# Difference attention in a two-block network: 64-row score matmuls of two units in one group, and the first softmax division on the output

## The chip, the cores and the metric

One core of a Trainium2 chip runs the whole network in one launch. The metric is the device time of that core in microseconds (us). TensorE (PE in the profile) multiplies, VectorE (DVE) and ScalarE (ACT) do the elementwise work, GpSimd (POOL) some sums, and SyncE (SP) issues the transfers of weights.

## What is computed

The program is a block of first kind (feed-forward, RWKV time mix, dilated attention, feed-forward) and then two layers of a second kind, each with an mLSTM branch, a difference attention branch, a Fourier branch, and a feed-forward. The change touches the difference attention branch of the two layers alone:

```python
def _diff_attn_core(q, k, v, lam):
    s = jnp.einsum('bqhmd,bkhmd->bhmqk', q, k).astype(jnp.float32) * (DA_DH ** -0.5)
    p = jax.nn.softmax(s, axis=-1)
    a = p[:, :, 0] - lam * p[:, :, 1]
    return jnp.einsum('bhqk,bkhe->bqhe', a.astype(v.dtype), v)
```

There are 8 heads of 2 x 64 columns of queries and keys (m = 0 and 1) and 128 columns of values. 256 tokens x attend to all 512 keys (x and context); in layer 0 the 256 context tokens attend to the 256 context keys too. All is float32.

## The kernel before, in words

Each engine has its own hand-written program; they meet at semaphores. A `Tally` counts them: `t.wait(name)` waits for one more count, `t.step(ins)` and `t.out(ins, name)` issue an instruction, raise a semaphore and wait for it, so that each engine goes strictly in its written order.

A unit is one head and one block of 128 queries (`units`). Layer 0 has 32 units, in which key widths of 512 and 256 alternate (query blocks 0, 2, 1, 3 of a head); layer 1 has 16 units, all 512 wide. For each unit n:

- PE, `da_scores`: two matmuls with 64 rows, m = 0 on rows 0 to 63 into bank n % 2, m = 1 on rows 64 to 127 into bank 4 + n % 2. They raise "scores". Before unit n they wait for "probs_in" of unit n - 2, which read the same banks.
- DVE, `da_in`: two maxima over the row (L3801) and a scaling by -0.125 (L3802), "weights_out".
- ACT, `exp` for m = 0 and m = 1 (L2725): the exponential out of PSUM into `DA_P`, with the row's sum by an accumulator read. After m = 1, "probs_in".
- DVE, `da_mid`: reciprocal of both sums (L3810), second weights by its reciprocal and by the factor lambda (L3811), first weights by theirs, plus the second (L3812), "probs".
- PE, `da_turn`: 4 or 2 transposes into bank 2 (L1143), "pt_psum". ACT, L2746: the copy of it out of bank 2, "pt_ready". PE, `da_values`: 4 or 2 matmuls into bank 6 + n % 2, "pv_psum". DVE, L3822: the copy of the 128x128 output, "pv_out".

A float32 matmul has two records in the profile, so "x4" of the scores is one unit, and x8 with x4 are the values and transposes of a 512-wide unit. Between these steps PE makes matmuls of the next gate (`fill`, one of 512 columns in layer 0, two of 256 in layer 1 per unit; 4 tiles in all, drained by ACT at L2341). PE's order in step n: scores n, fill, values n - 3, transposes n - 2. DVE's: `da_in` n, `da_mid` n - 1, copy n - 3. ACT's: exp(n, 0), copy of the transposes n - 2, exp(n, 1). Ahead of the loop stands the last product of the value projection (`end_units`, 16 records of 256 columns), which PE makes behind the scores of unit 0; ACT writes out its last tile and loads the exponential's table before exp(0, 0). Behind the loop PE waits for the last copy of the output before it goes on, and DVE and ACT normalize the output.

Of the kernel before, what the change touches and what calls it, by code (L numbers as in the profile page):

```python
# [18 lines left out]
P = 128  # L19
# [517 lines left out]
def program(nc, x_in, ctx_in, wide_in, down_in, par_in, const_in, const1_in, const2_in, out, dbg=None):  # L537
    with ExitStack() as ctx:
# [33 lines left out]
        bank = [ctx.enter_context(nc.psum_tensor(f"bank{b}", [P, 512], F32)) for b in range(8)]  # L572
# [562 lines left out]
        def _(pe):  # L1135
# [322 lines left out]
            def end_units(keys):  # L1458
                product(keys[-1], "P4")
# [444 lines left out]
            for la in range(2):  # L1904
# [122 lines left out]
                def da_scores(n):  # L2027
                    h, q = units[n]
                    k0, k1 = keys_of(q)
                    if n >= 2:  # L2030
                        t.wait("probs_in")
                    for m in range(2):
                        rows = slice(64 * m, 64 * m + 64)
                        last = matmul(bank[4 * m + n % 2][:, 0:(k1 - k0) * P], qT[rows, h, q * P:(q + 1) * P], kT[rows, h, k0 * P:k1 * P])
                    last.then_inc(S["scores"], 1)
# [23 lines left out]
                for n in range(len(units) + 3):  # L2059
                    if n == 0:  # L2060
                        pe.wait_ge(S["act_out"], ST[p + "da_v"].act_end - 1)
                    if n < len(units):
                        da_scores(n)
                        if n == 0:
                            end_units(run)
                        fill(per)
                    if n >= 3:
                        da_values(n - 3)
                    if 2 <= n < len(units) + 2:
                        da_turn(n - 2)  # L2070
# [125 lines left out]
        def _(act):  # L2196
# [438 lines left out]
            for la in range(2):  # L2635
# [86 lines left out]
                def exp(n, m, w):  # L2722

                    sc = stat[:, 4 * (n % 3):4 * (n % 3) + 4]
                    ins = af(DA_P(n, m)[:, 0:w], bank[4 * m + n % 2][:, 0:w], ACT.Exp, scale=0.125, bias=sc[:, m:m + 1],  # L2725
                             accum_out=sc[:, 2 + m:3 + m])
                    if m == 0:
                        t.step(ins)
                    else:
                        t.out(ins, "probs_in")  # L2730

                for n in range(n_units + 2):
                    if n < n_units:
                        w = 512 if DA_ORDER[qtiles][n % qtiles] < 2 else 256
                        if (n + 1) % (n_units // 4) == 0:
                            tile = (n + 1) // (n_units // 4) - 1
                            filled(ST[p + "da_gate0"], tile, DA_GATES0[:, tile, 0:nq], bank[3][:, 0:nq])
                        t.wait("weights_out")
                        exp(n, 0, w)
                    if n >= 2:  # L2740
                        k = n - 2
                        w = 512 if DA_ORDER[qtiles][k % qtiles] < 2 else 256
                        t.wait("pt_psum")
                        if k >= 2:
                            act.wait_ge(S["pv_psum"], PV_DA[la] + k - 1)
                        t.out(af(DA_PT(k)[:, 0:w], bank[2][:, 0:w], ACT.Copy), "pt_ready")  # L2746
                    if n < n_units:
                        exp(n, 1, 512 if DA_ORDER[qtiles][n % qtiles] < 2 else 256)
                act.wait_ge(S["act_out"], ST[p + "da_gate0"].act_end)

                def da_squares():
# [126 lines left out]
        def _(dve):  # L2878
# [731 lines left out]
            for la in range(2):  # L3610
# [185 lines left out]
                def da_in(n):  # L3796
                    w = 512 if units[n][1] < 2 else 256
                    sc = stat[:, 4 * (n % 3):4 * (n % 3) + 4]
                    t.wait("scores")
                    for m in range(2):  # L3800
                        t.step(nc.vector.tensor_reduce(sc[:, m:m + 1], bank[4 * m + n % 2][:, 0:w], axis=AX.X, op=ALU.max))  # L3801
                    t.out(ts(sc[:, 0:2], sc[:, 0:2], -0.125, None, mul), "weights_out")  # L3802

                def da_mid(n):

                    w = 512 if units[n][1] < 2 else 256
                    sc = stat[:, 4 * (n % 3):4 * (n % 3) + 4]
                    p0, p1 = DA_P(n, 0)[:, 0:w], DA_P(n, 1)[:, 0:w]
                    t.wait("probs_in")
                    t.step(nc.vector.reciprocal(sc[:, 2:4], sc[:, 2:4]))  # L3810
                    t.step(ts(p1, p1, sc[:, 3:4], lam[:, 2:3], mul, mul))  # L3811
                    t.out(stt(p0, p0, sc[:, 2:3], p1, mul, add), "probs")  # L3812

                for n in range(len(units) + 3):
                    if n < len(units):
                        da_in(n)
                    if 1 <= n < len(units) + 1:
                        da_mid(n - 1)
                    if n >= 3:
                        h, q = units[n - 3]  # L3820
                        t.wait("pv_psum")
                        t.out(copy(y3[:, q, h * P:(h + 1) * P], bank[6 + (n - 3) % 2][:, 0:P]), "pv_out")  # L3822
                say("dve_for_act")
                run = RUNS[2]
                t.wait("act_for_dve")
# [513 lines left out]
```

## Time and profile before

| what | value |
|---|---|
| median of 3 runs | 3066.15 us (3064.68 to 3066.62) |
| span of the profiled execution | 3068.6 us |
| PE, DVE, ACT busy over the span | 2994.5, 1778.7, 598.7 us (98%, 58%, 20%) |
| loop of layer 0 (first scores to last output copy) | 1420.8 to 1525.0 us |
| loop of layer 1 | 2619.2 to 2683.7 us |

The profiled execution has no device time of its own beside its span; the span is 0.08% above the median of the runs. Busy time counts an instruction from its start to its end. Matmuls overlap each other, so their starts tell more than their lengths. In a timeline row "[1.94 <-DVE small L3802]" is the idle time ahead of the instruction and what ended it.

### The profile page before, as it was taken

The page shows a single profiled execution, that of the slowest core. Times are in us where ns is not written, and L with a number is a line of the kernel's source. Part 1 is how long each engine was busy: PE and PEld are TensorE (multiplying, and loading weights), DVE is VectorE, ACT ScalarE, POOL GpSimd, SP SyncE. Part 2 cuts the span into 40 slices and gives each one's busy share as a digit, 9 for nine tenths or more (in the row PEclk, how much of TensorE's full clock was granted, in tenths as well). Part 3 has the DMA queues.
Part 4 walks back from the last instruction along what each step waited for, and adds up shares of the span by engine and source line. Part 5 has one row for each costly group of instructions (what it writes and reads, how often), then busy time and mean ns, then how long its engine had stood idle before and what let it go on. Part 6 is the DMA issues. An engine that isn't in the chain of part 4 may idle for free.

```text
span 3068.6 us, 37635 instructions
## 1 busy us (share of the span) xinstructions
PE 2994.5 (98%) x15352; PEld 2256.1 (74%) x15352; DVE 1778.7 (58%) x2602; ACT 598.7 (20%) x1182; POOL 535.9 (17%) x214
## 2 busy tenths in 40 slices
PE   8999999999999999999999999999999999999998
PEld 4448898775458757887588888888888888678543
DVE  6984642647766556657853268777324513742574
ACT  2103212212121112113611131111021200511110
POOL 4330000023332101221021212211110001010332
PEclk9999999999999999999999999999999999999999
DMA  6663301345543302442021234443232143133453
GB/s 264 234 233 137 138 30 44 123 180 180 181 184 129 112 28 76 144 133 94 29 87 65 83 144 152 150 143 137 98 124 92 60 158 115 58 151 130 162 175 126
DMA packets 57115, 389.86 MB, mean 127 GB/s; under 512 B 9072, under 2 KB 23408, under 8 KB 36336
## 3 DMA queue, kind: packets, MB, share of 16 engines
q1 hardware_dynamic: 52592, 383.27, 34.6%
q10 hardware_dynamic: 4352, 4.20, 0.7%
q8 instruction: 122, 2.00, 0.3%
q14 instruction: 49, 0.40, 0.0%
HBM read 373.53 MB, written 1.05 MB: 122 GB/s over the span
## 4 chain that ended last, share of the span: by engine, by line
PE 85%; DVE 7%; issue 6%; ACT 2%; POOL 0%; DMA 0%; DVEq 0%; SPq 0%; ACTq 0%; POOLq 0%
PE bank L1140 84%; DVE weights L3143 1%; PE bank L1143 1%; DVE arena L3472 0%; DVE factors L3156 0%; DVE factors L3051 0%; ACT h_T L2247 0%; DVE weights L3146 0%; DVE h_T L3245 0%; DVE arena L2990 0%; DVE arena L3173 0%; DVE masks L3941 0%; DVE arena L3506 0%; DVE small L3801 0%; DMA params<-params_dram 0%
## 5 line engine op out<-in xcount | busy, mean ns | idle before, releaser
L1140 PE MATMUL bank<-h_T,weights 128*128 128x256 f32 (+1 forms) x3184 | 780.6, 397 | 14.4 <-ACT arena L2364 3.1
L1140 PEld LDWEIGHTS bank<-h_T,weights 128*128 128x128 f32 x3184 | 601.2, 191 | 151.8 <-issue 65.1
L2862 POOL TENSOR_TENSOR weights<-weights 128x1024 f32<-128x1024 f32 (+2 forms) x105 | 272.5, 2596 | 1290.1 <-DMA weights<-wide_slabs_dram 1191.7
L2873 POOL TENSOR_TENSOR factors<-weights 128x1024 f32<-128x1024 f32 (+2 forms) x105 | 265.5, 2528 | 1214.4 <-PE bank L1140 992.8
L1140 PE MATMUL bank<-arena,weights 128*128 128x256 f32 x1784 | 393.9, 379 | 2.5 <-DVE arena L3173 0.9
L1140 PEld LDWEIGHTS bank<-arena,weights 128*128 128x128 f32 x1784 | 337.9, 190 | 51.4 <-issue 1.8
L1140 PE MATMUL bank<-factors,weights 128*128 128x256 f32 x1432 | 325.4, 381 | 5.0 <-DVE arena L3173 3.9
L1140 PE MATMUL bank<-weights,h_T 128*128 128x256 f32 (+2 forms) x1000 | 323.4, 470 | 4.1 <-DMA weights<-wide_slabs_dram 2.1
L1140 PE MATMUL bank<-weights,factors 128*128 128x256 f32 (+1 forms) x960 | 312.7, 470 | 4.1 <-DVE factors L3156 2.1
L1140 PEld LDWEIGHTS bank<-factors,weights 128*128 128x128 f32 x1432 | 272.7, 191 | 43.7 <-DVE arena L3173 5.1
L1140 PEld LDWEIGHTS bank<-weights,h_T 128*128 128x128 f32 x1000 | 190.3, 191 | 117.9 <-issue 89.8
L3143 DVE TENSOR_TENSOR weights<-weights,factors 128x1024 f32<-128x1024 f32 (+2 forms) x104 | 136.4, 1312 | 232.8 <-PE bank L1140 202.5
L1140 PEld LDWEIGHTS bank<-weights,factors 128*128 128x128 f32 x960 | 181.5, 190 | 118.9 <-issue 98.3
L3146 DVE TENSOR_TENSOR weights<-weights,factors 128x1024 f32<-128x1024 f32 (+2 forms) x104 | 130.4, 1254 | 168.5 <-PE bank L1140 167.0
L2357 ACT ACTIVATE arena<-bank 128x512 f32<-128x512 f32 (+1 forms) x144 | 83.3, 579 | 694.3 <-PE bank L1140 604.8
L1140 PE MATMUL bank<-factors 128*128 128x256 f32 (+3 forms) x816 | 212.7, 413 | 0.0
L3173 DVE TENSOR_TENSOR arena<-bank,arena 128x512 f32<-128x512 f32 (+1 forms) x132 | 88.1, 667 | 195.1 <-PE bank L1140 192.2
L1140 PE MATMUL bank<-arena 64*64 64x64 f32 (+7 forms) x1544 | 176.5, 307 | 11.0 <-ACT arena L2746 6.4
L1140 PEld LDWEIGHTS bank<-factors 128*128 128x128 f32 (+1 forms) x816 | 148.9, 190 | 50.6 <-issue 33.8
L1140 PE MATMUL bank<-weights,arena 128*128 128x512 f32 x396 | 175.0, 593 | 4.6 <-DVE weights L3143 4.6
L1140 PEld LDWEIGHTS bank<-arena 64*64 64x64 f32 (+2 forms) x1544 | 124.9, 162 | 52.9 <-issue 23.8
L3941 DVE SCALAR_TENSOR_TENSOR masks<-arena 128x1024 f32<-128x1024 f32 x88 | 152.5, 1732 | 2.9
(392 smaller groups left out, 2693.7 us busy)
## 6 DMA issues: line engine op xcount, KB each, us to landing
weights<-wide_slabs_dram SPq DMA_DIRECT2D x143, 2048.0 KB, 7.8
arena<-wide_slabs_dram SPq DMA_DIRECT2D x61, 512.0 KB, 4.2
weights<-down_slabs_dram SPq DMA_DIRECT2D x8, 1408.0 KB, 5.8
merged_T<-arena SPq DMA_DIRECT2D x240, 32.0 KB, 1.9
merged_T<-wide_slabs_dram SPq DMA_DIRECT2D x15, 512.0 KB, 4.5
x_T<-wide_slabs_dram SPq DMA_DIRECT2D x11, 512.0 KB, 9.3
arena<-arena ACTq DMA_DIRECT2D x16, 256.0 KB, 10.1
weights<-wide_slabs_dram SPq DMA_DIRECT2D x3, 1024.0 KB, 5.1
```

The lines of the kernel that those rows point to most:

```text
L1140: return mm(out, lhsT, rhs, start=start, stop=stop, skip_group_check=True)
L1143: return nc.tensor.transpose(out, in_, ident[0:in_.shape[0], 0:in_.shape[0]])
L2357: af(place(u)[into], bank_of(u, of), ACT.Copy, scale=scale).then_inc(S["snapped"], 1)
L2862: nc.gpsimd.tensor_tensor(b[2], b[2], b[3], ALU.add).then_inc(S["first_sums"], 1)
L2873: nc.gpsimd.tensor_tensor(e, b[2], b[0], ALU.subtract).then_inc(S["first_sums"], 1)
L3143: ins = tt(b[0], b[3], e, sub)
L3146: ins = tt(b[1], b[1], e, sub)
L3173: ins = stt(dst, src, 1.0 / 16, dst, mul, add) if "ml_k" in u.name else tt(dst, src, dst, add)
L3941: ins = stt(ADA_PRODUCT, ada_tile(b), 1.0, COND_ROWS[:, s * D:(s + 1) * D], mul, mul, accum_out=ada_all[:, column:column + 1])
```

## The change

PE issues the scores of units n and n + 1 (n even) in one group, and waits for "probs_in" of both units before (n - 2 and n - 1) ahead of the group. At the start both first units stand ahead of `end_units`. ACT makes exp(n, 0) and exp(n, 1) one behind the other, and the copy of the transposes n - 2 behind them; the drain of a gate tile moves behind the exponentials too. DVE makes `da_in` of two units, then an output copy, `da_mid` of the two, and another output copy. In `da_mid` the multiplication of the whole second weights (L3811) goes; in its place comes an operation on one column (lambda times the second reciprocal times the first sum), and the addition takes that column as its factor. The output is divided by the first sum in its copy out of PSUM (tensor_scalar in place of copy); the reciprocals lie in 6 places of `stat` until then.

```diff
--- before.py
+++ after.py
@@ -2027,8 +2027,6 @@
                 def da_scores(n):
                     h, q = units[n]
                     k0, k1 = keys_of(q)
-                    if n >= 2:
-                        t.wait("probs_in")
                     for m in range(2):
                         rows = slice(64 * m, 64 * m + 64)
                         last = matmul(bank[4 * m + n % 2][:, 0:(k1 - k0) * P], qT[rows, h, q * P:(q + 1) * P], kT[rows, h, k0 * P:k1 * P])
@@ -2060,9 +2058,13 @@
                     if n == 0:
                         pe.wait_ge(S["act_out"], ST[p + "da_v"].act_end - 1)
                     if n < len(units):
-                        da_scores(n)
-                        if n == 0:
-                            end_units(run)
+                        if n % 2 == 0:
+                            if n:
+                                t.wait("probs_in", 2)
+                            da_scores(n)
+                            da_scores(n + 1)
+                            if n == 0:
+                                end_units(run)
                         fill(per)
                     if n >= 3:
                         da_values(n - 3)
@@ -2732,11 +2734,12 @@
                 for n in range(n_units + 2):
                     if n < n_units:
                         w = 512 if DA_ORDER[qtiles][n % qtiles] < 2 else 256
+                        t.wait("weights_out")
+                        exp(n, 0, w)
+                        exp(n, 1, w)
                         if (n + 1) % (n_units // 4) == 0:
                             tile = (n + 1) // (n_units // 4) - 1
                             filled(ST[p + "da_gate0"], tile, DA_GATES0[:, tile, 0:nq], bank[3][:, 0:nq])
-                        t.wait("weights_out")
-                        exp(n, 0, w)
                     if n >= 2:
                         k = n - 2
                         w = 512 if DA_ORDER[qtiles][k % qtiles] < 2 else 256
@@ -2744,8 +2747,6 @@
                         if k >= 2:
                             act.wait_ge(S["pv_psum"], PV_DA[la] + k - 1)
                         t.out(af(DA_PT(k)[:, 0:w], bank[2][:, 0:w], ACT.Copy), "pt_ready")
-                    if n < n_units:
-                        exp(n, 1, 512 if DA_ORDER[qtiles][n % qtiles] < 2 else 256)
                 act.wait_ge(S["act_out"], ST[p + "da_gate0"].act_end)
 
                 def da_squares():
@@ -3807,19 +3808,29 @@
                     sc = stat[:, 4 * (n % 3):4 * (n % 3) + 4]
                     p0, p1 = DA_P(n, 0)[:, 0:w], DA_P(n, 1)[:, 0:w]
                     t.wait("probs_in")
-                    t.step(nc.vector.reciprocal(sc[:, 2:4], sc[:, 2:4]))
-                    t.step(ts(p1, p1, sc[:, 3:4], lam[:, 2:3], mul, mul))
-                    t.out(stt(p0, p0, sc[:, 2:3], p1, mul, add), "probs")
-
-                for n in range(len(units) + 3):
+                    t.step(nc.vector.reciprocal(da_rows(n), sc[:, 2:4]))
+                    t.step(stt(sc[:, 3:4], da_rows(n)[:, 1:2], lam[:, 2:3], sc[:, 2:3], mul, mul))
+                    t.out(stt(p0, p1, sc[:, 3:4], p0, mul, add), "probs")
+
+                def da_rows(n):
+                    return stat[:, 16 + 2 * (n % 6):18 + 2 * (n % 6)]
+
+                def da_out(n):
+                    h, q = units[n]
+                    t.wait("pv_psum")
+                    t.out(ts(y3[:, q, h * P:(h + 1) * P], bank[6 + n % 2][:, 0:P], da_rows(n)[:, 0:1], None, mul), "pv_out")
+
+                for n in range(0, len(units) + 4, 2):
                     if n < len(units):
                         da_in(n)
-                    if 1 <= n < len(units) + 1:
-                        da_mid(n - 1)
-                    if n >= 3:
-                        h, q = units[n - 3]
-                        t.wait("pv_psum")
-                        t.out(copy(y3[:, q, h * P:(h + 1) * P], bank[6 + (n - 3) % 2][:, 0:P]), "pv_out")
+                        da_in(n + 1)
+                    if 3 <= n < len(units) + 3:
+                        da_out(n - 3)
+                    if n < len(units):
+                        da_mid(n)
+                        da_mid(n + 1)
+                    if 2 <= n < len(units) + 2:
+                        da_out(n - 2)
                 say("dve_for_act")
                 run = RUNS[2]
                 t.wait("act_for_dve")
```

The places on which the prediction rests, as the programs stand. PE in layer 0, from the first scores (banks 0 and 4 are the scores of a 512-wide unit, banks 1 and 5 of a 256-wide one, bank 3 the fill or `end_units`, bank 2 transposes, banks 6 and 7 values). Before:

```order
L1140 MATMUL bank3<-h_T,weights 128x512
L1140 MATMUL bank6<-arena 128x128 x4
L1143 MATMUL bank2<-common,arena 128x128 x2
L1140 MATMUL bank0<-arena 128x512
L1140 MATMUL bank4<-arena 128x512
L1140 MATMUL bank3<-h_T,weights 128x512
L1140 MATMUL bank7<-arena 128x128 x2
L1143 MATMUL bank2<-common,arena 128x128 x4
L1140 MATMUL bank1<-arena 128x256
L1140 MATMUL bank5<-arena 128x256
```

and now:

```order
L1140 MATMUL bank0<-arena 128x512
L1140 MATMUL bank4<-arena 128x512
L1140 MATMUL bank1<-arena 128x256
L1140 MATMUL bank5<-arena 128x256
L1140 MATMUL bank3<-h_T,weights 128x512
L1140 MATMUL bank7<-arena 128x128 x2
L1143 MATMUL bank2<-common,arena 128x128 x4
L1140 MATMUL bank3<-h_T,weights 128x512
L1140 MATMUL bank6<-arena 128x128 x4
L1143 MATMUL bank2<-common,arena 128x128 x2
```

Here a matmul is one row, not two records. The same ten stand in one pair of units; the scores of the second have moved ahead by a fill, values and transposes.

ACT in layer 0, from the table load (banks 0 and 4, then 1 and 5, are read by the exponentials; bank 2 by the copy of the transposes). Before:

```order
L2725 ACT_TABLE_LOAD
L2725 ACTIVATE arena,small<-bank0,small 128x512
L2725 ACTIVATE arena,small<-bank4,small 128x512
L2725 ACTIVATE arena,small<-bank1,small 128x256
L2725 ACTIVATE arena,small<-bank5,small 128x256
L2725 ACTIVATE arena,small<-bank0,small 128x512
L2746 ACTIVATE arena<-bank2 128x512
L2725 ACTIVATE arena,small<-bank4,small 128x512
L2725 ACTIVATE arena,small<-bank1,small 128x256
L2746 ACTIVATE arena<-bank2 128x256
L2725 ACTIVATE arena,small<-bank5,small 128x256
```

and now:

```order
L2727 ACT_TABLE_LOAD
L2727 ACTIVATE arena,small<-bank0,small 128x512
L2727 ACTIVATE arena,small<-bank4,small 128x512
L2727 ACTIVATE arena,small<-bank1,small 128x256
L2727 ACTIVATE arena,small<-bank5,small 128x256
L2727 ACTIVATE arena,small<-bank0,small 128x512
L2727 ACTIVATE arena,small<-bank4,small 128x512
L2749 ACTIVATE arena<-bank2 128x512
L2727 ACTIVATE arena,small<-bank1,small 128x256
L2727 ACTIVATE arena,small<-bank5,small 128x256
L2749 ACTIVATE arena<-bank2 128x256
```

The copy of the transposes has moved from between the two exponentials of a unit to behind them, so one copy stands between the exponentials of the two units of a group.

## Rows read from the trace of the kernel before

**Rows 1.** Busy time by engine in the two loops; columns as printed, clock as share.
```profile
core 0: us, PE busy (x) PEld busy (x) DVE busy (x) ACT busy (x) POOL busy (x), PEclk, DMA share, GB/s
1420.80:1525.10 104.30, 99.50 (x497) 56.19 (x497) 90.04 (x227) 62.11 (x166) 2.49 (x1) 1.00 0.11 41
2619.20:2683.80 64.60, 60.26 (x337) 41.35 (x336) 52.18 (x114) 37.79 (x86) 0.00 (x0) 1.00 0.18 66
```

**Rows 2.** Timeline (start us, us, engine, line, operation), layer 0, one pair.
```profile
1479.02 1.42 DVE L3801 TENSOR_REDUCE small<-bank 128x1 f32<-128x512 f32 x2
...
1480.59 0.70 PE L1140 MATMUL bank<-arena 64*128 64x256 f32 x4
...
1481.22 1.13 PE L1140 MATMUL bank<-h_T,weights 128*128 128x512 f32 x2
...
1484.94 0.69 DVE L3801 TENSOR_REDUCE small<-bank 128x1 f32<-128x512 f32 x1
```

**Rows 3.** Timeline, layer 0, first units of the loop.
```profile
1427.54 0.69 ACT L2725 ACTIVATE arena<-bank,small 128x512 f32<-128x512 f32 x1
...
1429.18 1.13 PE L1140 MATMUL bank<-arena 64*128 64x512 f32 x4
...
1429.40 0.47 ACT L2725 ACTIVATE arena<-bank,small 128x256 f32<-128x256 f32 x1 [0.27 <-DVE small L3802]
...
1430.00 0.47 ACT L2725 ACTIVATE arena<-bank,small 128x256 f32<-128x256 f32 x1
...
1430.79 1.41 DVE L3801 TENSOR_REDUCE small<-bank 128x1 f32<-128x512 f32 x2
...
1432.50 0.69 ACT L2725 ACTIVATE arena<-bank,small 128x512 f32<-128x512 f32 x1 [1.94 <-DVE small L3802]
...
1433.31 0.60 ACT L2746 ACTIVATE arena<-bank 128x512 f32<-128x512 f32 x1
...
1433.94 0.69 ACT L2725 ACTIVATE arena<-bank,small 128x512 f32<-128x512 f32 x1
...
1435.27 0.70 PE L1140 MATMUL bank<-arena 64*128 64x512 f32 x2
```

**Rows 4.** Timeline, layer 1, first units of the loop.
```profile
2625.84 1.13 PE L1140 MATMUL bank<-arena 64*128 64x512 f32 x4
2625.97 0.69 ACT L2725 ACTIVATE arena<-bank,small 128x512 f32<-128x512 f32 x1
...
2627.08 1.42 DVE L3801 TENSOR_REDUCE small<-bank 128x1 f32<-128x512 f32 x2 [4.97 <-PE bank L1140]
...
2627.96 1.13 PE L1140 MATMUL bank<-arena 64*128 64x512 f32 x4
```

**Rows 5.** Timeline of DVE, layer 1, the second half of one unit.
```profile
2638.37 0.17 DVE L3810 RECIPROCAL small<-small 128x2 f32<-128x2 f32 x1
...
2638.57 0.55 DVE L3811 TENSOR_SCALAR arena<-arena,small 128x512 f32<-128x512 f32 x1
...
2639.15 0.75 DVE L3812 SCALAR_TENSOR_TENSOR arena<-arena,small 128x512 f32<-128x512 f32 x1
...
2639.82 0.28 DVE L3822 COPY arena<-bank 128x128 f32<-128x128 f32 x1
```

**Rows 6.** Timeline of PE, an earlier stage: 64-row matmuls of two widths together.
```profile
578.54 0.93 PE L1140 MATMUL bank<-factors 64*128 64x128 f32 x8
579.39 0.70 PE L1140 MATMUL bank<-arena,weights 128*128 128x256 f32 x2
```

**Rows 7.** Timeline of PE and DVE, last score pairs and last output copies.
```profile
1513.34 1.13 PE L1140 MATMUL bank<-arena 64*128 64x512 f32 x4
...
1524.72 0.29 DVE L3822 COPY arena<-bank 128x128 f32<-128x128 f32 x1 [1.16 <-PE bank L1140]
...
2669.36 1.13 PE L1140 MATMUL bank<-arena 64*128 64x512 f32 x4
...
2683.44 0.29 DVE L3822 COPY arena<-bank 128x128 f32<-128x128 f32 x1 [2.04 <-PE bank L1140]
```

**Rows 8.** Busy time by engine around a fall of TensorE's clock; columns as in rows 1.
```profile
390.00:392.00 2.00, 0.85 (x16) 0.61 (x12) 1.93 (x6) 0.00 (x0) 0.00 (x0) 1.00 0.03 8
...
394.20:397.60 3.40, 3.40 (x60) 3.40 (x58) 1.42 (x4) 0.55 (x1) 0.00 (x0) 0.50 0.00 0
```

## The prediction

> **What bounds the kernel now.** I first read the busy times of the two loops [rows 1]. PE is busy 99.5 of 104.3 us in layer 0 and 60.3 of 64.6 us in layer 1, DVE 90.0 and 52.2 us, ACT about 60% of each. So two engines are nearly full, and the loops are a close race. The timeline decides it. In layer 0 a pair of units (512 and 256 keys wide) takes 5.92 us from maximum to maximum on DVE (1479.02 to 1484.94) [rows 2], and DVE has no gap in between: DVE bounds layer 0. In layer 1 the scores of units 2 and 14 start at 2627.96 and 2669.36 [rows 4, 7], 41.40 us for 12 units, 3.45 us for one and 6.90 us for a pair; there PE goes from group to group without a wait and DVE's unit is just as full. Both loops hide all hand-overs between engines behind work of other units. A change that regroups units must keep that cover, so I read the hand-overs too [rows 3, 4].
>
> **What is taken from PE.** A group of two 64-row matmuls of 256 columns takes 0.63 us up to the fill (1480.59 to 1481.22) [rows 2]. Where matmuls of 128 and of 256 columns with 64 rows stand together, both take 0.85 us (578.54 to 579.39) [rows 6]: the 128 wide ones add 0.22, a quarter of the 0.85, where they are a third of the columns. So a second group behind a first pays its columns alone; a group has a fixed 0.2 us (0.63 less twice 0.22). I take 0.2 us as the low end and 0.4 us (as much again at its neighbours, an estimate by doubling) as the high end per group saved. 24 groups go: 4.8 to 9.6 us of PE work. The Trainium skill, page TensorEngine Tiling (Array Packing), section Key Properties, says that a change of the tiling mode drains TensorE; by that rule alone the change can only win, and the time would be that of the first rival below.
>
> **What is taken from DVE.** The scaling of the second weights goes, 0.58 us from its start to the next (2638.57 to 2639.15) [rows 5], in the 256-wide units less. A one-column operation comes; the nearest row is the reciprocal of two columns, 0.20 us to the next start [rows 5]. The output copy (0.28 us [rows 5]) becomes a multiplication by a column; I take it at the same time, and up to 0.07 us more for the range. Net some 0.3 us per unit, 24 x 2 units: 14 us of DVE work. It is worth nothing unless DVE sets the pace, and I find that it no longer does.
>
> **What is added: a longer ring.** Scores of units n and n + 1 now wait until both units before are through both exponentials, and nothing of a later unit is under way in the meantime. I follow the ring from one group's start to the next in layer 0, with n 512 wide and n + 1 256 wide:
>
> - scores of n start, to the first maximum: 1.24 us (2625.84 to 2627.08, DVE was idle) [rows 4];
> - first maximum to the first exponential: 1.71 us (1430.79 to 1432.50, ACT was idle) [rows 3];
> - both exponentials of n, one behind the other: 2 x 0.81 = 1.62 us (1432.50 to 1433.31) [rows 3];
> - the copy of the transposes n - 2, which now stands right here, then values n - 2 and transposes n - 1, and the next scores: 1.96 us (1433.31 to 1435.27, the same shapes in the same order) [rows 3].
>
> The sum is 6.53 us. The other branch of the last step is the copy (0.63, 1433.31 to 1433.94) and the exponentials of n + 1 (2 x 0.60, 1429.40 to 1430.00) [rows 3], about 1.85 us, so values and transposes end last by 0.1. The maximum of n + 1 on DVE ends long before ACT comes to it. PE's and DVE's own work per pair is some 5.5 us, less than the ring. So layer 0 goes from 5.92 to 6.53 us per pair. Group starts from unit 2 to unit 30 are 14 rings, 91.4 us, against 84.2 us before (1429.18 to 1513.34) [rows 3, 7]: **+7.2 us**.
>
> In layer 1 all units are 512 wide, and the ring runs through DVE: exponentials of n, copy, exponentials of n + 1: 1.62 + 0.63 + 1.59 = 3.84 us; a hand-over of 0.1 us (an estimate, the smallest gaps between engines here); reciprocal 0.20, one-column operation 0.20, addition 0.67 (2639.15 to 2639.82), output copy 0.32 [rows 5]; then maximum to exponential, 1.71. That is 7.04 us against 6.90. Six rings give 42.2 against 41.4 us: **+0.8 us**.
>
> **Start and end of the loops.** The first two score groups now stand ahead of the value projection's last product, which delays that product, and by it ACT's table load and exp(0, 0), by 0.43 us in layer 0 (two 64-row steps of 0.22) and by 0.86 us in layer 1, where the unit is 512 wide. Before, scores 2 started at 1429.18 and 2627.96. Now they wait for the exponentials of units 0 and 1: 1427.54 + 0.43 + 1.62 + 1.20 gives 1430.8, and 2625.97 + 0.86 + 3.24 gives 2630.1 [rows 3, 4]: **+1.6 and +2.1 us**. At the end of layer 0, from scores 30 to the last output copy, it was 11.4 us (1513.34 to 1524.72) [rows 7]. Now exp(31) ends after 1.24 + 1.71 + 1.62 + 0.63 + 1.17 = 6.4 us, the gate drain and the copy of transposes 29 (half as wide, 0.2 us shorter) come to 7.4, then values 29 with transposes 30 (1.3 us), a round of 1.96, and copy 31 with values 31 (1.3): 12.0 us, **+0.6**. In layer 1 the same laying out gives 14.0 us against 14.1 (2669.36 to 2683.44) [rows 7]: **0**. PE waits for the last output copy before it goes on, so all of it reaches the end of the program; outside the loops nothing changes.
>
> Sum: 7.2 + 0.8 + 1.6 + 2.1 + 0.6 = 12.3, rounded up for the small terms to 12.5 us. The profiled execution's span of 3068.6 would become 3081; against the median of 3066.15 I say **3078.6 us**.
>
> **The rivals.**
>
> *PE sets the pace, and the change wins.* If ACT's results come before PE asks for them, the pair costs PE 0.4 us less, 5.5 us in layer 0 and 6.5 in layer 1, and DVE is lighter still. Then 24 x 0.4 = 9.6 us go: 3056.6 us. It decides if the ring of layer 0 is below 5.9 us; I find 6.53, each part a start-to-start time. For it speaks that both full engines lose work. Chance 0.08.
>
> *The copy of the transposes does not count.* If it fell into ACT's idle time ahead of the exponentials, the ring would lose 0.63 us: 5.9 in layer 0, 6.4 in layer 1 (there PE's 6.5 decides, a gain of 2.4), and with the longer start the time is about 3068, no difference. Against it: ACT's order is fixed, the transposes n - 2 come behind the group and a fill on PE, later than the first exponential, and at 1433.94 the exponential starts only behind the copy though its unit had long been ready [rows 3]. Chance 0.10.
>
> *PE's clock falls.* Before, the loops ran at a granted clock of 1.00 [rows 1]. At 390 to 392 us PE was busy 0.85 of 2.00 us, and at 394.2 to 397.6 the granted clock was 0.50 [rows 8], the lower level, 1.2 GHz. The new wait ahead of scores 2 leaves PE idle some 2 us in each layer, and in the ring it is busy about five sixths of the time. One such fall costs up to 1.7 us where PE is in the ring; two of them 3.4: 3082. Chance 0.12.
>
> *The second group pays its fixed cost after all.* Then scores n + 1 come 0.2 us later, under the 1.4 us of maxima of unit n: no difference in time, only in the trace.
>
> **How the numbers follow.** My forecast has the rest, 0.70. Slower are the forecast and the clock's case, 0.82; within 0.2% (6.1 us, about what a measurement of this kernel can tell) is the second rival, 0.10; faster the first, 0.08. The range takes in a shorter ring (6.42 by the exponentials' branch alone, -1.5 us) and a start that costs nothing (-3.7) at the low end, and two falls of the clock and a dearer output copy at the high end: 3072 to 3083. Both other cases are below it, 0.18 together.
>
> **What would show it.** Group starts 6.5 us apart in layer 0 and 7.0 in layer 1; PE idle about 1 us ahead of the values (released by ACT's copy) in each pair; DVE waiting for ACT ahead of the second reciprocal; first groups at 1430.8 and some 10 us later than now in layer 1; no L3811 of full width. I am wrong if group starts are under 6.0 us apart in layer 0, and then it is the ring that failed.

## The result, and the profile after

| kernel | median (runs) | ratio to before, 95% interval |
|---|---|---|
| before | 3065.41 us (3063.09 to 3066.93, 6) | |
| changed | 3076.70 us (3072.50 to 3078.59, 6) | 1.0033 [1.0024, 1.0043] |

The change costs 11.3 us by the medians; the ratio of 1.0033 is 10.1 us, with an interval of 7.4 to 13.2. The forecast was 3078.6 us, in a range of 3072 to 3083. The profiled execution of the changed kernel took 3077.47 us. Its page and its two loops:

```profile
span 3075.7 us, 37642 instructions
PE 2987.1 (97%) x15352; PEld 2253.7 (73%) x15352; DVE 1772.6 (58%) x2602; ACT 595.2 (19%) x1182; POOL 534.6 (17%) x214
```

Busy time by engine, one loop a row, columns as in [rows 1]:

```profile
1417.20:1529.00 111.80, 95.06 (x497) 57.23 (x497) 85.21 (x227) 60.27 (x166) 2.35 (x1) 1.00 0.11 38
2624.20:2690.90 66.70, 58.96 (x337) 41.56 (x337) 48.71 (x114) 36.13 (x86) 0.00 (x0) 1.00 0.18 64
```

PE has 4.4 us and DVE 4.8 us less to do in layer 0 than in [rows 1], as meant, and the loop takes 7.5 us longer: both engines now wait. The waits of the layer 0 loop (engine and line, what it waited for, us in total, times, longest) name the place. First before, then after:

```profile
PEld bank L1140 <- ACT arena L2746: 15.1, 19, 1.6
PE bank L1140 <- ACT arena L2746: 3.5, 6, 0.8
```

```profile
PEld bank L1140 <- ACT arena L2749: 26.4, 18, 2.0
...
PE bank L1140 <- ACT arena L2749: 13.3, 18, 1.2
```

PE's wait for ACT's copy of the transposes grew from 3.5 to 13.3 us, that of its weight loads from 15.1 to 26.4 us. One pair of units of layer 0, all engines (start, length, engine, line, operation), shows the ring:

```profile
1452.96 1.56 PE L1140 MATMUL bank<-arena 64*128 64x512 f32 x8
...
1454.20 1.42 DVE L3802 TENSOR_REDUCE small<-bank 128x1 f32<-128x512 f32 x2
...
1454.45 1.13 PE L1140 MATMUL bank<-h_T,weights 128*128 128x512 f32 x2
...
1455.92 0.69 ACT L2727 ACTIVATE arena<-bank,small 128x512 f32<-128x512 f32 x1 [2.42 <-DVE small L3803]
...
1456.73 0.69 ACT L2727 ACTIVATE arena<-bank,small 128x512 f32<-128x512 f32 x1
...
1457.41 0.59 ACT L2749 ACTIVATE arena<-bank 128x512 f32<-128x512 f32 x1
...
1458.05 1.16 PE L1140 MATMUL bank<-arena 128*128 128x128 f32 x8 [0.73 <-ACT arena L2749]
...
1459.29 0.17 DVE L3811 RECIPROCAL small<-small 128x2 f32<-128x2 f32 x1 [0.48 <-ACT arena L2727]
...
1459.35 0.70 PE L1140 MATMUL bank<-arena 64*128 64x512 f32 x2
```

From group to group it is 6.39 us (1452.96 to 1459.35). Its legs: scores to maximum 1.24, maximum to exponential 1.72, both exponentials 1.49, and from the copy by way of the values to the next group 1.94. The other way to that group, through the exponentials of the 256-wide unit, was ready some 0.1 us earlier: in experiment 4, where PE waits for them, the group starts 0.62 us behind the start of the last of them (1472.21 to 1472.83), which here would be 1458.62 + 0.62 = 1459.24 where the group starts at 1459.35. It is a close race. PE stands idle 0.73 us ahead of the values and DVE 0.48 us ahead of the second reciprocal. The start and the end of the loops, layer 0 and then layer 1:

```profile
1417.19 1.56 PE L1140 MATMUL bank<-arena 64*128 64x512 f32 x8
...
1427.04 1.56 PE L1140 MATMUL bank<-arena 64*128 64x512 f32 x8 [1.91 <-ACT arena L2727]
...
1516.91 1.56 PE L1140 MATMUL bank<-arena 64*128 64x512 f32 x8
...
1528.56 0.35 DVE L3821 TENSOR_SCALAR arena<-bank,small 128x128 f32<-128x128 f32 x1 [1.10 <-PE bank L1140]
...
2624.25 1.99 PE L1140 MATMUL bank<-arena 64*128 64x512 f32 x8
...
2634.96 1.99 PE L1140 MATMUL bank<-arena 64*128 64x512 f32 x8 [2.33 <-ACT arena L2727]
...
2676.74 1.99 PE L1140 MATMUL bank<-arena 64*128 64x512 f32 x8
...
2690.45 0.35 DVE L3821 TENSOR_SCALAR arena<-bank,small 128x128 f32<-128x128 f32 x1 [1.98 <-PE bank L1140]
```

From here on "the loops" are the times from the first scores to the last output copy of each layer, and "a pair" is the time between the scores of units n and n + 2 (n even, so 512 wide in layer 0). They are read from the profiled execution of each kernel:

| kernel | pair, layers 0 / 1 | loops, layers 0 / 1 | sum against before |
|---|---|---|---|
| before | 5.92 / 6.90 | 103.91 / 64.20 | |
| changed | 6.40 / 7.01 | 111.37 / 66.20 | +9.5 |

The spans of the two profiled executions differ by 7.1 us only, since the one of before came to its first scores 3.6 us later (1420.81 against 1417.19) over the same instructions. That is why the loops are compared, and the medians, but not the spans.

### The profile page after: what moved, and what is told of

Its sections match the earlier page's. It is cut to its first block, busy times and chain, and to the rows that moved or that the text cites. A ratio compares the mean times of both kernels' runs of the same rounds, so it can differ in the third digit from the quotient of the medians.

```text
span 3075.7 us, 37642 instructions
## 1 busy us (share of the span) xinstructions
PE 2987.1 (97%) x15352; PEld 2253.7 (73%) x15352; DVE 1772.6 (58%) x2602; ACT 595.2 (19%) x1182; POOL 534.6 (17%) x214
## 4 chain that ended last, share of the span: by engine, by line
PE 43%; issue 5%; DVE 1%; ACT 1%; POOL 0%; DVEq 0%; ACTq 0%; POOLq 0%
PE bank L1140 43%; ACT h_T L2249 0%; DVE masks L3952 0%; DVE factors L3157 0%; DVE weights L3144 0%; POOL factors L2874 0%; PE bank L1143 0%; DVE arena L3174 0%; DVE arena L3856 0%; DVE weights L3147 0%; POOL weights L2863 0%; DVE factors L4041 0%; DVE arena L4037 0%; DVE h_T L2933 0%; DVE arena L3757 0%
## 5 line engine op out<-in xcount | busy, mean ns | idle before, releaser
L1140 PE MATMUL bank<-arena 64*64 64x64 f32 (+7 forms) x1544 | 170.2, 303 | 26.4 <-ACT arena L2749 17.1
## 6 DMA issues: line engine op xcount, KB each, us to landing
arena<-arena ACTq DMA_DIRECT2D x16, 256.0 KB, 10.1
```

Of the source, the lines that this page charges most:

```text
L1140: return mm(out, lhsT, rhs, start=start, stop=stop, skip_group_check=True)
```

## The experiments

The kernel before was run again beside them: its median was 3067.10 us beside experiments 1 to 4 and 3066.60 us beside 5 to 8, and the ratios are against these runs.

What had to be told apart: whether the ring (the theory), PE's work or DVE's work sets the pair; whether the copy of the transposes counts; and which of the change's three parts (PE's grouping, ACT's order, the arithmetic) makes the loss.

**1. The order without the arithmetic.** The changed kernel with the old `da_mid` and the old output copy.

```diff
-                    t.step(stt(sc[:, 3:4], da_rows(n)[:, 1:2], lam[:, 2:3], sc[:, 2:3], mul, mul))
-                    t.out(stt(p0, p1, sc[:, 3:4], p0, mul, add), "probs")
+                    t.step(ts(p1, p1, sc[:, 3:4], lam[:, 2:3], mul, mul))
+                    t.out(stt(p0, p0, sc[:, 2:3], p1, mul, add), "probs")
```

> The changed order on all engines with the old arithmetic (full-width scaling of the second weights, plain output copy). Ring theory (the group waits for exponentials, copy of the transposes, values and transposes, and DVE has slack in layer 0): the added DVE work of about 0.3 us a unit shows in layer 0 for less than 0.1 us a pair (6.40 to about 6.48), in layer 1, where DVE is in the ring, for 0.26 a pair (7.02 to about 7.3); in all 2 to 3 us slower than the change, some 12 to 14 us slower than before. Rival (DVE's total work sets the pace): 48 units x 0.26 = 12 us slower than the change.

Measured: 3077.64 us, ratio 1.0042 [1.0027, 1.0058]; pairs 6.46 and 7.28 to 7.29 us. PE in each layer:

```profile
1469.23 1.56 PE L1140 MATMUL bank<-arena 64*128 64x512 f32 x8
...
1475.69 0.70 PE L1140 MATMUL bank<-arena 64*128 64x512 f32 x2
```

```profile
2647.32 1.99 PE L1140 MATMUL bank<-arena 64*128 64x512 f32 x8
...
2654.60 0.70 PE L1140 MATMUL bank<-arena 64*128 64x512 f32 x2
```

With all of DVE's old work back, the pair grows by 0.06 us in layer 0, where DVE is not in the ring, and by 0.27 in layer 1, where it is. The median is 0.9 us above that of the changed kernel, where the rival wanted 12. So in the new order DVE's work is not the bound of layer 0, and the order alone makes the loss.

**2. The arithmetic without the order.** The changed kernel with the loops of before on PE, ACT and DVE (PE's and ACT's as in before, DVE's `da_in` n, `da_mid` n - 1, output n - 3).

```diff
-                for n in range(0, len(units) + 4, 2):
+                for n in range(len(units) + 3):
                     if n < len(units):
                         da_in(n)
...
+                    if 1 <= n < len(units) + 1:
+                        da_mid(n - 1)
+                    if n >= 3:
                         da_out(n - 3)
```

> The old order on all engines with the new arithmetic. Ring theory: PE's own work bounds both loops, 5.8 us a pair in layer 0 (5.92 before, where DVE was full) and 6.9 in layer 1 as before; 2 to 3 us faster than before, 3062 to 3063. Rival (DVE's work sets the pace): 48 x 0.26 = 12 us faster. Rival (the arithmetic itself, with its column in the output copy, costs the time): slower than before.

Measured: 3063.89 us, ratio 0.9993 [0.9984, 1.0002]; pairs 5.79 and 6.90, loops 101.87 and 63.52. PE in layer 0, from the scores of one 512-wide unit to the next:

```profile
1464.87 1.13 PE L1140 MATMUL bank<-arena 64*128 64x512 f32 x4
...
1470.66 0.70 PE L1140 MATMUL bank<-arena 64*128 64x512 f32 x2
```

PE is idle nowhere in this pair: it takes over as the bound, 0.13 us below DVE's 5.92. The lighter DVE is worth 2.0 us in the loop of layer 0 and 0.7 in that of layer 1, and no more, because PE stands right behind it. The medians alone do not show the gain: their interval holds 1.

**3. A shorter copy, in the changed order.** ACT copies the first 128 columns of the transposes alone. The rest of the copy is left out, so the values of the other columns are stale.

```diff
-                        t.out(af(DA_PT(k)[:, 0:w], bank[2][:, 0:w], ACT.Copy), "pt_ready")
+                        t.out(af(DA_PT(k)[:, 0:P], bank[2][:, 0:P], ACT.Copy), "pt_ready")
```

> The change, but ACT copies only the first 128 columns of the transposes out of PSUM, so values of the other columns are stale. Ring theory: the copy stands in the ring, and 0.3 us less of it (0.63 to about 0.31 for a 512-wide unit) makes the pair 6.4 to 6.1 us in layer 0 and 7.0 to 6.7 in layer 1: 5 us off in layer 0, 2 to 3 in layer 1, 7 to 8 us faster than the change. Rival (the wait for both units' exponentials alone sets the pace, or PE does): no difference.

Measured: 3068.88 us, ratio 1.0010 [1.0001, 1.0019]; pairs 6.08 and 6.70.

```profile
1466.24 1.56 PE L1140 MATMUL bank<-arena 64*128 64x512 f32 x8
...
1470.69 0.27 ACT L2749 ACTIVATE arena<-bank 128x128 f32<-128x128 f32 x1
...
1470.99 0.47 ACT L2727 ACTIVATE arena<-bank,small 128x256 f32<-128x256 f32 x1
1471.01 1.16 PE L1140 MATMUL bank<-arena 128*128 128x128 f32 x8 [0.41 <-ACT arena L2749]
...
1472.32 0.70 PE L1140 MATMUL bank<-arena 64*128 64x512 f32 x2
```

The copy takes 0.30 us to the next start (1470.69 to 1470.99) where it took 0.62 (1457.41 to 1458.03 in the changed kernel), and both the pair (6.40 to 6.08) and PE's idle time (0.73 to 0.41) shrink by that 0.32. In layer 1 the pair shrinks by 0.31. What is taken off the copy comes off the pair in full; the median is 7.8 us below that of the changed kernel, where 7 to 8 were expected.

**4. The copy out of the ring.** PE keeps the group of two but makes the transposes of unit n - 2 at once behind it, ahead of the fill; ACT makes that copy while DVE takes the maxima. DVE makes both output copies behind the four maxima. Of the edit only PE's loop is shown; the orders of all three engines change together here, so this run does not tell which of them the gain needs.

```diff
+                        da_scores(n)
+                        da_scores(n + 1)
...
+                    if 2 <= n < len(units) + 2:
+                        da_turn(n - 2)
                     if n < len(units):
                         fill(per)
-                    if n >= 3:
+                    if 3 <= n < len(units) + 3:
                         da_values(n - 3)
+                    if n < len(units):
+                        fill(per)
+                    if 1 <= n < len(units) + 1:
+                        da_turn(n - 1)
                     if 2 <= n < len(units) + 2:
-                        da_turn(n - 2)
+                        da_values(n - 2)
```

> The change with the copy of the transposes taken out of the ring: PE makes the transposes of n - 2 right behind the group of scores, ACT copies them ahead of the exponentials of n, in what was idle time, and the transposes of n - 1 behind the exponentials of n + 1; DVE takes both output copies between the maxima and the additions. Ring theory: only maxima and exponentials are left in the ring (5.8 us in layer 0, 6.1 in layer 1), so PE's own work decides: 5.8 us a pair in layer 0 and 6.6 in layer 1; 12 to 14 us faster than the change, 2 to 4 us faster than before. Rival (the longer wait for two units is the cause, wherever the copy stands): as slow as the change.

Measured: 3059.16 us, ratio 0.9975 [0.9966, 0.9983], 7.9 us below the median of before beside it and 17.5 us below that of the changed kernel; pairs 5.66 and 6.46, loops 100.26 and 62.47. That is more than the 2 to 4 and 12 to 14 us expected. Both pairs are shorter than expected (5.8 and 6.6), which explains part of it; the two loops give 5.4 us of the 7.9, and where the rest lies is not shown. Layer 0, all engines (L2735 is the exponential here, L2747 the copy):

```profile
1467.17 1.56 PE L1140 MATMUL bank<-arena 64*128 64x512 f32 x8
...
1468.42 1.42 DVE L3815 TENSOR_REDUCE small<-bank 128x1 f32<-128x512 f32 x2
...
1469.41 0.60 ACT L2747 ACTIVATE arena<-bank 128x512 f32<-128x512 f32 x1 [1.52 <-issue]
...
1470.13 0.69 ACT L2735 ACTIVATE arena<-bank,small 128x512 f32<-128x512 f32 x1
...
1470.94 0.69 ACT L2735 ACTIVATE arena<-bank,small 128x512 f32<-128x512 f32 x1
...
1471.62 0.46 ACT L2735 ACTIVATE arena<-bank,small 128x256 f32<-128x256 f32 x1
...
1472.83 0.30 PEld L1140 LDWEIGHTS bank<-arena 64*128 64x128 f32 x4 [0.26 <-ACT arena L2735]
```

The copy now lies in ACT's idle time, and the ring is scores, maximum (1.25), exponential (1.71), two exponentials (1.49), two shorter ones and the next group (1.21): 5.66 us. In layer 1 PE goes on without idle time; from one fill to the same fill two groups later:

```profile
2646.66 1.03 PE L1140 MATMUL bank<-h_T,weights 128*128 128x256 f32 x4
...
2653.12 1.03 PE L1140 MATMUL bank<-h_T,weights 128*128 128x256 f32 x4
```

There the saved group comes through: 6.46 us against 6.90 with single groups (experiment 2), 0.44 us a pair. Part of it stands at PE's neighbours: the fill takes 0.87 us up to the next matmul (2646.66 to 2647.53) with transposes ahead of it, where in experiment 2 it took 0.97 (2642.71 to 2643.68) with scores ahead of it. The Trainium skill, page TensorEngine Tiling (Array Packing), section Key Properties, says that a change of the tiling mode drains TensorE. No row here shows the drain itself; that fewer changes make PE's pair 0.44 us shorter agrees with it, and it is time saved only where PE is the bound.

**5. The second unit's scores behind the value projection.** Experiment 4, with `end_units` between the scores of unit 0 and of unit 1, against the late start.

```diff
                         da_scores(n)
-                        da_scores(n + 1)
                         if n == 0:
                             end_units(run)
+                        da_scores(n + 1)
```

> e4 with the scores of unit 1 behind the value projection's last product instead of ahead of it. That product, ACT's table load and exp(0, 0) come 0.43 us earlier in layer 0 and 0.86 us earlier in layer 1; the second group waits for the exponentials of units 0 and 1 as before. Expected by the sum of the prediction's start term: first group to second 9.4 us in place of 9.85 and 9.8 in place of 10.7; about 1 us faster than e4, which only the trace can tell. If the start is bound by something else, no difference in those two distances.

Measured: 3059.72 us, ratio 0.9981 [0.9972, 0.9990]; loops 99.67 and 61.57.

```profile
1412.79 1.13 PE L1140 MATMUL bank<-arena 64*128 64x512 f32 x4
1413.85 3.72 PE L1140 MATMUL bank<-weights,factors 128*128 128x256 f32 x16
1417.50 0.70 PE L1140 MATMUL bank<-arena 64*128 64x256 f32 x4
...
1422.21 0.70 PE L1140 MATMUL bank<-arena 64*128 64x512 f32 x2 [1.91 <-ACT arena L2735]
```

Scores 2 come 9.42 us behind the first in layer 0 and 9.85 in layer 1, where experiment 4 had 9.85 and 10.70. So the delay of the last product is real, 0.43 and 0.85 us, as the forecast had it. The medians can't tell the two kernels apart; a gain of 1.3 us is below what they resolve.

**6. The changed kernel with single groups on PE.** Only PE's loop is the old one.

```diff
-                        if n % 2 == 0:
-                            if n:
-                                t.wait("probs_in", 2)
-                            da_scores(n)
-                            da_scores(n + 1)
-                            if n == 0:
-                                end_units(run)
+                        if n >= 2:
+                            t.wait("probs_in")
+                        da_scores(n)
+                        if n == 0:
+                            end_units(run)
```

> The change with the scores ungrouped on PE alone (scores of n behind those of n - 2 as before, one group of 64-row matmuls per unit); ACT and DVE keep the changed order. Ring theory: the copy behind both exponentials and the wait for values and transposes set the pair even without the group: 6.4 us in layer 0, and in layer 1 7.0 to 7.9 because the maxima of n + 1 come later; as slow as the change or up to 3 us slower. Rival (holding the scores back until both older units are done is what costs): back to the time of before, 3067, or less.

Measured: 3081.05 us, ratio 1.0056 [1.0042, 1.0069]; pairs of 6.40 in layer 0, of 7.02 and 7.95 in layer 1.

```profile
1464.20 1.13 PE L1140 MATMUL bank<-arena 64*128 64x512 f32 x4
...
1469.29 1.16 PE L1140 MATMUL bank<-arena 128*128 128x128 f32 x8 [0.34 <-ACT arena L2747]
...
1470.60 0.70 PE L1140 MATMUL bank<-arena 64*128 64x512 f32 x2
```

Giving the grouping up wins nothing back, and in layer 1 it costs more; the median is 4.4 us above that of the changed kernel, where up to 3 were expected. Nor does it save the start: scores 2 come 8.36 us behind the first, as before, but scores 4 come 16.71 us behind the first (with the clock at half in about the last 2 us), against 16.54 in the changed kernel and 14.46 before. With or without the group the pair of layer 0 is 6.40 us; without it PE only waits less (0.34 in place of 0.73). So it is not PE's double wait ahead of the group that costs.

**7. ACT's order alone, in the kernel before.**

```diff
+                        t.wait("weights_out")
+                        exp(n, 0, w)
+                        exp(n, 1, w)
                         if (n + 1) % (n_units // 4) == 0:
...
-                        t.wait("weights_out")
-                        exp(n, 0, w)
```

> The kernel before with one edit: ACT makes both exponentials of a unit and then the copy of the transposes (and the gate drain). Ring theory: the copy comes 0.8 us later, values, transposes and the next scores behind it on PE too: about 6.4 us a pair in layer 0, 6.9 to 7.2 in layer 1; 8 to 10 us slower than before. Rival (grouping on PE or the paired order on DVE is the cause): no difference from before.

Measured: 3076.33 us, ratio 1.0036 [1.0023, 1.0049]; pair of layer 0 6.40 us, in layer 1 6.90 to 7.33.

```profile
1466.89 0.59 ACT L2747 ACTIVATE arena<-bank 128x512 f32<-128x512 f32 x1
...
1467.53 1.16 PE L1140 MATMUL bank<-arena 128*128 128x128 f32 x8 [0.34 <-ACT arena L2747]
```

This one edit, with the old arithmetic and the old orders of PE and DVE, costs about as much as the whole change (9.7 us by the medians), though not place by place: the start of layer 0 is 8.37 us as before, and from scores 2 to scores 14 of layer 1 it loses 1.9 us (43.30 against 41.40), the changed kernel 0.4. In its layer 1 the clock was at half for 10 us behind that, so that loop's 69.49 us is not used. ACT's order is enough to lose the time; the changed kernel with ACT's old order was not run, so what PE's group and DVE's order would cost or win beside that order stays open.

**8. Experiment 4 with the old arithmetic.** The order of experiment 4, `da_mid` and the output copy of before.

```diff
-                    t.step(stt(sc[:, 3:4], da_rows(n)[:, 1:2], lam[:, 2:3], sc[:, 2:3], mul, mul))
-                    t.out(stt(p0, p1, sc[:, 3:4], p0, mul, add), "probs")
+                    t.step(ts(p1, p1, sc[:, 3:4], lam[:, 2:3], mul, mul))
+                    t.out(stt(p0, p0, sc[:, 2:3], p1, mul, add), "probs")
```

> e4 with the old arithmetic. DVE's work is then 0.2 to 0.3 us more a unit: DVE is full at 5.9 us a pair in layer 0 and at 6.85 in layer 1, as before. The order alone is worth nothing then, the arithmetic alone about 2 us (e2), both together 6 to 8 (e4): expected 1 us slower to 1 us faster than before. If the grouping had a worth of its own, the pair would be at 5.7 and 6.5 here too.

Measured: 3064.62 us, ratio 0.9998 [0.9989, 1.0007]; pairs 5.92 and 6.85.

```profile
1466.70 0.17 DVE L3824 RECIPROCAL small<-small 128x2 f32<-128x2 f32 x1
...
1472.62 0.17 DVE L3824 RECIPROCAL small<-small 128x2 f32<-128x2 f32 x1
```

DVE is full again, 5.92 us from one reciprocal to the same one of the next pair, as in [rows 2]. So neither part of the good version does it alone. The pairs show it best: 5.79 and 6.90 us with the arithmetic alone, 5.92 and 6.85 with the order alone, 5.66 and 6.46 with both. In the medians the arithmetic alone has a ratio of 0.9993 [0.9984, 1.0002] (experiment 2), the order alone one of 0.9998 [0.9989, 1.0007], both together one of 0.9975 [0.9966, 0.9983].

## Why the prediction was right

**The bound.** It rested on a ring in place of two full engines. Shown: group starts 6.40 and 7.01 us apart where 6.53 and 7.04 were said; PE idle 0.73 us ahead of the values, released by ACT's copy, where about 1 was said (the ring was shorter, and PE's own work was not 5.5 us a pair but 6.39 - 0.73 = 5.66); DVE waiting for ACT ahead of the second reciprocal; and no bound by DVE's work (experiment 1) or by PE's (experiment 6).

**The terms.** Read from the rows of the changed kernel above against [rows 3, 4, 7]:

| term | said | measured |
|---|---|---|
| layer 0, scores 2 to scores 30 | +7.2 | 89.87 - 84.16 = +5.7 |
| layer 1, scores 2 to scores 14 | +0.8 | 41.78 - 41.40 = +0.4 |
| start, layers 0 and 1 | +1.6, +2.1 | 9.85 - 8.37 = +1.5, 10.71 - 8.72 = +2.0 |
| end, layers 0 and 1 | +0.6, 0 | 11.65 - 11.38 = +0.3, 13.71 - 14.08 = -0.4 |
| sum | +12.3 | +9.5; medians +11.3 [7.4, 13.2] |

**The mis-sized term** is the leg "both exponentials of n, one behind the other: 2 x 0.81". It measured 1.49 us (1455.92 to 1457.41): what follows the first exponential starts 0.81 us behind it (1455.92 to 1456.73), but what follows the second starts after 0.68 (1456.73 to 1457.41). The row that I took the 0.81 from, 1432.50 to 1433.31 [rows 3], is that of a first exponential with a copy behind it, and I doubled it. The other legs of the ring were right to 0.02 us. 14 rings x 0.13 = 1.8 us too much; of this, 0.3 us came back by the first ring, which took 6.69 us (1427.04 to 1433.73) and not 6.39, and that leaves the gap of 1.5 us in that term. The start terms have the same 0.13 in them.

In layer 1 the hit of 7.01 us is partly luck. The exponentials were 0.13 us too long there too, but the one-column operation took 0.26 us and not 0.20 (2655.94 to 2656.20), and the output copy 0.38 and not 0.32 (2656.87 to 2657.25); both stand in that ring, and the errors nearly cancel. That the term came out at +0.4 and not +0.8 is mostly the first ring, 6.71 us.

Between the loops' +9.5 and the medians' +11.3 lie 1.8 us that have no place in the two profiles. They lie inside the interval, and against the 10.1 us of the ratio the gap is 0.6. The clock does not explain the loss: the mean granted clock of the profiled executions was 0.994 before and 0.995 after.

**Small prices.** The output copy with a column measured 0.35 us, my upper end (0.28 plus 0.07). The one-column operation takes 0.25 us to the next start (1457.81 to 1458.06), not 0.20; in layer 0 it is outside the ring. The 14 us of DVE work were too many: DVE's busy time in the two loops fell by 8.3 us (90.04 to 85.21 and 52.18 to 48.71). In the forecast they were worth nothing, so the sum does not suffer.

**The first rival** (PE sets the pace, the change wins) fell here, but its mechanism is real: its condition, a ring below PE's own time, is met in layer 1 by experiment 4, where the pair is shorter by about the 0.4 us that I took as the high end for a saved group. Inside the group it was 0.20 us (two units 1.49 us, 1452.96 to 1454.45, against 1.06 + 0.63 singly), the low end; the rest comes at its neighbours.

**The second rival** (the copy doesn't count) fell by experiments 3 and 7. The argument against it, that the transposes stand behind the group and a fill, was also what to mend: moved ahead of the fill, the copy does fall into the idle time, and the kernel is faster than before.

**The clock** stayed at 1.00 in both loops of the profiled change. It fell in some of the others, below.

**The last rival** (the second group pays its fixed cost) fell too: the two groups of layer 0 take 1.49 us together, 0.20 less than singly.

## What to carry to other kernels

Before work of two units is put together, follow the ring from one group's start to the next, leg by leg by start times: an engine near 95% busy stops being the bound as soon as the ring is longer than its work. Take every price from a row in which the operation stands at the place that it will have; a first exponential did not have the price of a second one. On an engine that goes strictly in its order, a short copy that others wait for costs its whole length when it is put behind the long operations (here 0.32 us of pair for 0.32 us of copy), and nothing when it is put into the wait ahead of them. Look for such a copy before giving up on a change whose parts all save work; here the cure was an order of steps and not less arithmetic, yet it needed the arithmetic to pay.

## What was not expected of the hardware

Two spacings on ACT, with the same accumulator read behind both exponentials. Behind the first 512-wide exponential of a unit the next operation starts after 0.81 us, be it an exponential (1455.92 to 1456.73) or, before, a copy (1432.50 to 1433.31 [rows 3]). Behind the second it starts after 0.68 us, be it a copy (1456.73 to 1457.41) or, in experiment 4, an exponential (1470.94 to 1471.62). So it is not the following operation that makes the difference. The program has the first raise and wait for ACT's own semaphore (`t.step`) and the second "probs_in" (`t.out`); whether that is the cause is not shown.

TensorE's clock fell at different places from execution to execution. In the changed kernel and in experiment 1 PE waits 1.91 us ahead of the second group of layer 0. From 1.4 us behind the start of that group (1427.04 and 1423.54), first the changed kernel and then experiment 1, columns as in [rows 1]:

```profile
1428.40:1432.00 3.60, 2.56 (x10) 1.07 (x8) 3.43 (x6) 1.96 (x5) 1.95 (x1) 1.00 0.18 73
```

```profile
1425.00:1428.40 3.40, 3.40 (x9) 1.92 (x8) 3.23 (x7) 1.63 (x5) 1.83 (x1) 0.51 0.19 77
```

The clock stayed up in the one and was at half in the other. In experiment 7 it was at half for longer, behind the last scores of layer 1:

```profile
2682.00:2692.00 10.00, 8.03 (x31) 6.61 (x30) 0.94 (x4) 3.00 (x3) 0.00 (x0) 0.50 0.25 107
```

So a loop time of one execution can carry some us of half clock (those of experiments 1 and 3 to 7 do), and the pair times, read in stretches at 1.00, are the safer reading. What decides in which execution the clock falls stays open; no run here varied it by itself.
